# Three seven-product pairs in six of fifteen weight groups, and the other pairs at tiles 2 and 10

## The chip, the cores and the metric

The kernel runs on one core of a Trainium2 chip. The metric is the device time of one execution in microseconds (us). Names used below: TensorE (PE in the profile, PEld its weight loads), VectorE (DVE), ScalarE (ACT), GpSimd (POOL) and SyncE (SP), which issues the weight loads.

## The reference, cut to what matters

One encoder block on 256 tokens of width 2048, all in float32. The part that the change touches is the squared-ReLU MLP at the end:

```python
h = h + (g_mla * y_mla + g_fox * y_fox) @ w_out[l]
hn = rmsnorm(h, mlp_norm[l])
u = jnp.square(jax.nn.relu(hn @ w_up[l]))     # w_up: 2048 x 8192
h = h + u @ w_down[l]                         # w_down: 8192 x 2048
return rmsnorm(h, final_norm)
```

## The kernel before, in words

**Numbers in two parts.** Every operand of a product is split into a rounded part ("hi") and a rest ("lo"), and a product takes three matmuls: hi by hi, hi by lo, lo by hi (`three_passes`, L781 to L783). For a weight tile ScalarE writes hi (`unit_to_hi`, L1042) and VectorE then writes lo (`unit_to_lo`, L1318).

**Units and rings.** The weights are packed by the host as a stream of 456 units of 128 x 1024 values. SyncE loads them into a ring (`raw`, 4 slots, and from unit 208 on 8 slots with `raw_more`). hi and lo go to a ring `hl` of 4 slots, so hi of unit u starts only when TensorE has finished unit u-4. Each engine has a program written out by hand: VectorE and ScalarE walk over all units in order, and `make_due` lists, for each unit, which other work an engine does right after its own part of that unit. What is listed at a unit cannot overtake what stands ahead of it on its engine.

**Double groups.** The MLP is cut into four parts, each with two "up" groups (up0 0, up0 1, ...) and two "down" groups (the last part has one, then two ordinary groups). They are units 200 to 439: fifteen groups of 16 units, one 128-deep tile of the contraction per unit, and 1024 columns. For an ordinary tile TensorE computes four products (two token blocks by two column halves) into banks 0 to 3, twelve matmuls. The last two units of a group are worked block by block, and `block_left` and `unit_used` tell VectorE when each bank is finished.

**Seven-product pairs.** At the tiles named in `SEVEN` (4 and 10 before), two neighbouring tiles are taken together in Strassen's manner: seven products instead of eight, 21 matmuls instead of 24 (`seven_products`, L813). The order in it is: bank 7 and bank 5 (need the first two weight sums), bank 6 (third sum), bank 4 (needs unit k split), bank 1 (unit k), then banks 0 and 2 (need unit k+1 split). For a pair VectorE makes sums of the weight tiles (`weight_sums`, L1328, L1331, L1332), ScalarE their hi (`two_sums_to_hi` L1047, `third_sum_to_hi` L1052) and VectorE their lo (L1341). Both engines do this immediately ahead of their part of the pair's first unit. The sums have one buffer, which is free when bank 4's product of the previous pair is done. Sums of the activation rows of the pair's tiles are made once for each part (`row_sums`, L1353 to L1356, and hi and lo of them, L1126 and L1362), for the chunks of four tiles in `IN_CHUNK`, when these come back turned.

**The work after a group.** VectorE combines banks 4 to 7 at the group's units 14 and 15 ("products summed"; for down groups two more steps, at the next group's units 0 and 2). At the next group's unit 1 come the totals: `totals` (up) or `totals_into_resid` (down), the last of whose operations waits for the end of the group. After an up group ScalarE computes the squared ReLU of the two halves at the next group's unit 1 and unit 2 (`hidden_squares`, L1115 twice and L1120). VectorE transposes them in blocks at units 2 and 6 (`turn_hidden`, L1571), GpSimd sends each through HBM and back (L629, L636), and at units 8 and 12 they are split into `u_hl` (L1134, L1591), with row sums where the chunk has a pair.

**Start of the MLP.** Group up0 0 begins in banks 0 and 1, which the last w_out group has used. VectorE adds these to the residual in `take_tokens` (L1641), which is listed at unit 202, that is, after lo of unit 202.

Of the kernel before, what the change touches and what calls it, by code (L numbers as in the profile page):

```python
# [7 lines left out]
F32 = mybir.dt.float32  # L8
F32R = mybir.dt.float32r
# [67 lines left out]
        self.name, self.g = name, g  # L77


SEVEN = (4, 10)  # L80
IN_CHUNK = {k // 4: n for n, k in enumerate(SEVEN)}


def pairs_by_seven(name, g):

    return SEVEN


LAST_DOWN = f"down{MLP_PARTS - 1}"
# [138 lines left out]
def make_due():  # L228


    due = [[] for _ in range(N_UNITS)]

    def after(unit, what, g):
        due[min(unit + RING, N_UNITS - 1)].append((what, g))

    for gr in GROUPS:
        middle = gr.u0 + gr.units // 2 - 1
        if (gr.name, gr.g) in SCORES_IN:
            after(middle, "scored", SCORES_IN[gr.name, gr.g])
        if gr.name == "y_fox" and gr.g >= 2:  # L240
            after(middle, "mixed", 4 + gr.g)
        if gr.double:
            due[gr.u0 + 14].append(("p1 copied", gr))
            steps = (14, 15) if gr.name[:2] == "up" else (14, 15, 16, 18)
            for step, later in enumerate(steps):
                due[gr.u0 + later].append(("products summed", (gr, step)))
            due[gr.last + 2].append(("totals", gr))
        if gr.double and gr.name == LAST_DOWN:
            for c in range(2):
                due[gr.last + 3 + c].append(("chunk squared", Chunk(gr.name, 2 * gr.g + c)))  # L250
                due[gr.last + 5 + c].append(("chunk gained", Chunk(gr.name, 2 * gr.g + c)))
        if gr.name[:2] == "up":
            for c in range(2):
                piece = Chunk(gr.name, 2 * gr.g + c)
                piece.of, piece.c = gr, c
                due[gr.last + 2 + c].append(("hidden", piece))
                due[gr.last + 3 + 4 * c].append(("hidden turns", piece))
                due[gr.last + 9 + 4 * c].append(("u turned", piece))
                if piece.g in IN_CHUNK:
                    due[gr.last + 10 + 4 * c].append(("u summed", piece))  # L260
            if gr.n == 0:
                due[gr.u0 + 6].append(("mlp mean", gr))
                due[gr.u0 + 8].append(("mlp root", gr))
        if gr.double:
            continue
        if gr.name in ("y_mla", "w_out"):
            if gr.name == "w_out":
                after(gr.last + TURN_UNITS["w"] - 1, "h back", gr)
            after(gr.last + TURN_UNITS[gr.name[0]], {"y": "m turned", "w": "h turned"}[gr.name[0]], gr)
        if gr.name == "fq" and gr.g == 0:  # L270
            for later, what in ((2, "x norm"), (3, "latent norms"), (6, "keys rotated"), (9, "cq back"),
                                (10, "cq turned"), (14, "keys back"), (15, "keys turned"), (17, "forget exp"),
                                (18, "forget sums")):
                after(gr.u0 + later, what, gr)
        if gr is GROUPS[-1]:
            continue
        later = {("fq", 0): 5, ("fq", 1): 4, ("ukv_k", 0): 2, ("w_out", CHUNKS - 1): -1}.get((gr.name, gr.g), 0)
        after(gr.last + later - (gr.units == 1), "group", gr)
        if gr.name == "gates" and gr.g < 4:
            after(gr.last, "mixed", gr.g)  # L280
        elif gr.name == "gates" and gr.g == 7:
            after(gr.last, "mixed", 4)
        elif gr.name == "y_fox" and gr.g == 0:
            after(gr.last, "mixed", 5)
        elif gr.name in ("fq", "uq_nope"):
            after(gr.last + later + 8, "queries turned", gr)
        elif gr.name == "uq_rope":
            after(gr.last + 8, "queries rotated", gr)
            after(gr.last + 14, "queries turned", gr)
        elif gr.name == "fv" and gr.g == 1:  # L290
            after(gr.last, "scored", 0)
        elif gr.name == "ukv_v" and gr.g == 1:
            after(gr.last, "scored", 4)
    for work in due:
        work.sort(key=lambda it: not (it[0] == "group" and it[1].name == "w_out"))
    return due
# [45 lines left out]
def program(nc, stream, x_t, x_n, consts, gains, final_gain, cum_rows, prob_rows, turn_rows, out_n):  # L342
# [3 lines left out]
    def at(name, offset, *shape, dt=F32):  # L346
        return nc.alloc_sbuf_tensor_at(name, [P, *shape], dt, offset=sbuf0 + offset)
# [14 lines left out]
    prob_t = [at(f"prob_t{i}", o + offset * kib, 4, 2, 3, 32) for i, offset in enumerate((22, 15))]  # L362
    blocks = at("blocks", o + 19 * kib, TB * WIDE)
    hid = at("hid", o, 5, WIDE)
    sums = at("sums", o + 10 * kib, len(SEVEN), 4, 2, P)
    sums_hl = at("sums_hl", o + 10 * kib, len(SEVEN), 4, 2, P, dt=F32R)
    junk = at("junk", o + 23 * kib, WIDE)
    assert C_COUNT * 4 <= 8 * kib and G_COUNT * 4 <= 512
    A = o + 25 * kib
# [15 lines left out]
    m_hl = at("m_hl", B, KT, 2, T, dt=F32R)  # L385
    u_hl = at("u_hl", A, K_FF, 2, T, dt=F32R)
    raw_more = at("raw_more", B, DEEP_RING - RING, UNIT)
    u_sums = at("u_sums", B + 16 * kib, len(SEVEN), 4, 2, P)
    u_sums_hl = at("u_sums_hl", B + 16 * kib, len(SEVEN), 4, 2, P, dt=F32R)
    C = B + 32 * kib  # L390
    x_in = at("x_in", C, KT + KT * T)
    gate = at("gate", C, 2 * CHUNKS, TB, WIDE)
# [36 lines left out]
    with ctx:  # L429
# [110 lines left out]
        RIGHT_PIECES = [slice(2 * WIDE, 2 * WIDE + WIDE // 2), slice(2 * WIDE + WIDE // 2, 3 * WIDE),  # L540
                        slice(3 * WIDE, 4 * WIDE)]

        AHEAD_SUMS = {u for u in SEVEN_AT if u >= DEEP_FROM + DEEP_RING}

        def slot_of(u):
            return u % RING
# [15 lines left out]
        def sums_of(name):  # L562
            return {"up": sums_hl, "do": u_sums_hl}[name[:2]]
# [150 lines left out]
        def _(pe):  # L714
# [70 lines left out]
            def double_group(gr, tile, before_unit):  # L785
# [27 lines left out]
                def seven_products(k):  # L813

                    n = SEVEN.index(k)
                    last = k == gr.seven[-1]
                    sum_rows = lambda i: lambda part: sums_of(gr.name)[:, n, i, part]
                    sum_weights = lambda i: lambda part: (wsum_lo if part else wsum_hi)[:, i]
                    if gr.name == "up0":
                        pe.wait_ge(sums_split, n + 1)  # L820
                    elif gr.name[:2] == "do":
                        pe.wait_ge(sums_split, len(SEVEN) * (int(gr.name[4:]) + 1) + n + 1)
                    pe.wait_ge(wsum_split, 2 * SEVEN_AT[gr.u0 + k] + 1)
                    add_to(7, sum_rows(2), sum_weights(1), last)
                    add_to(5, sum_rows(0), sum_weights(0), last)
                    pe.wait_ge(wsum_split, 2 * SEVEN_AT[gr.u0 + k] + 2)
                    add_to(6, sum_rows(1), sum_weights(2), last)
                    pe.wait_ge(unit_split, gr.unit[k] + 1)
                    add_to(4, rows(k, 0), weights(k, 0), last).then_inc(seven_summed, 1)
                    add_to(1, rows(k + 1, 1), weights(k, 1)).then_inc(unit_used, 1)  # L830
                    pe.wait_ge(unit_split, gr.unit[k + 1] + 1)
                    add_to(0, rows(k + 1, 0), weights(k + 1, 1))
                    add_to(2, sum_rows(3), weights(k + 1, 0)).then_inc(unit_used, 1)
# [179 lines left out]
        def _(act):  # L1013
# [108 lines left out]
            def row_sums_to_hi(name, g):  # L1122

                n, (to, to_hl) = IN_CHUNK[g], ROW_SUMS[name[0]]
                act.wait_ge(sums_done, sums_before(name) + n + 1)
                nc.scalar.activation(to_hl[:, n, :, 0], to[:, n, :, 1], ACT.Copy).then_inc(sums_hi, 1)  # L1126

            def turned_to_hi(gr):
                back, dst, k0, tiles = turn_split(gr)
# [158 lines left out]
        def _(dve):  # L1288
# [55 lines left out]
            def row_sums(gr):  # L1344

                n, back = IN_CHUNK[gr.g], by_token(turned[:, SPLIT_NO[gr.name, gr.g] % 2])
                i = SEVEN[n] - 4 * gr.g
                to = lambda s: ROW_SUMS[gr.name[0]][0][:, n, s, 1].rearrange("p (a j) -> p a j", a=4)
                if gr.name in GAINED:
                    dve.wait_ge(turned_gained, GAINED[gr.name][0] + gr.g + 1)  # L1350
                else:
                    dve.wait_ge(turned_in, 4 * 16 * (TURN_NO[gr.name, gr.g] + 1))
                then_wait(nc.vector.tensor_tensor(to(0), back[:, i, 1], back[:, i + 1, 1], ALU.subtract))  # L1353
                nc.vector.tensor_tensor(to(2), back[:, i, 1], back[:, i, 0], ALU.subtract)
                then_wait(nc.vector.tensor_tensor(to(1), back[:, i, 0], to(0), ALU.subtract))
                nc.vector.tensor_tensor(to(3), back[:, i + 1, 0], to(1), ALU.subtract).then_inc(sums_done, 1)  # L1356

            def row_sums_to_lo(name, g):

                n, (to, to_hl) = IN_CHUNK[g], ROW_SUMS[name[0]]  # L1360
                dve.wait_ge(sums_hi, sums_before(name) + n + 1)
                nc.vector.tensor_tensor(to_hl[:, n, :, 1], to[:, n, :, 1], to_hl[:, n, :, 0].bitcast(F32),  # L1362
                                        ALU.subtract).then_inc(sums_split, 1)

            def sum_products(gr, step):
# [451 lines left out]
```

## Time and profile before

| | |
|---|---|
| median of 3 runs | 1267.52 us (1267.26 to 1268.73) |
| the profiled execution, as timed | 1264.23 us |
| its span in the trace | 1262.3 us |
| TensorE busy | 1250.6 us, 99% of the span, 5576 matmuls |
| TensorE weight loads busy | 1036.2 us, 82% |
| VectorE busy | 961.0 us, 76% |
| ScalarE busy | 670.4 us, 53% |
| GpSimd busy | 137.7 us, 11% |
| mean granted TensorE clock | 0.998 |

The profile is one execution. Its start-to-last-instruction span is 1.9 us shorter than its time, and its time is 3.3 us below the median of the runs. Busy time of an engine is the union of its instructions; the duration of one instruction can reach into the next one's, so the distance between starts tells more than the duration.

### The profile page before, as it was taken

What the parts mean: (1) busy time and instruction counts of PE and PEld (TensorE: products, weight loads), DVE (VectorE), ACT (ScalarE), POOL (GpSimd) and SP (SyncE); (2) the same over time, 40 slices, a digit from 0 to 9 for tenths busy, and PEclk for the clock granted to TensorE, in tenths of its full rate; (3) what the DMA queues carried; (4) which work ended last, traced back from release to release, by engine and by line L of the source; (5) the groups of instructions that cost most, each with busy time, mean ns of one, the idle gap of its engine ahead of it and who ended that gap; (6) DMA issues with size and microseconds to landing.
All of it is one profiled execution on the core that took longest, in us unless ns stands there. A gap on an engine that the chain in (4) does not pass through costs nothing.

```text
span 1262.3 us, 14832 instructions
## 1 busy us (share of the span) xinstructions
PE 1250.6 (99%) x5576; PEld 1036.2 (82%) x5576; DVE 961.0 (76%) x1057; ACT 670.4 (53%) x808; POOL 137.7 (11%) x239
## 2 busy tenths in 40 slices
PE   9999999999999999999999999999999999999997
PEld 7888888888888888887888888878888888888876
DVE  6676566646676677578899987889878897879884
ACT  6645345444555434455666445565455655456653
POOL 0021101103221112010001000110001110001100
PEclk9999999999999999999999999999999999999999
DMA  9788857765887779677787656766656786657761
GB/s 329 257 291 276 259 166 218 231 196 184 273 267 213 219 272 292 214 255 253 247 269 257 210 176 224 250 229 221 222 201 217 246 266 202 198 199 269 270 211 67
DMA packets 83143, 293.91 MB, mean 233 GB/s; under 512 B 11320, under 2 KB 12416, under 8 KB 82432
## 3 DMA queue, kind: packets, MB, share of 16 engines
q1 hardware_dynamic: 67536, 243.04, 58.0%
q0 software_dynamic: 14528, 48.00, 12.4%
q10 hardware_dynamic: 1008, 1.92, 0.5%
q8 instruction: 45, 0.74, 0.3%
q14 instruction: 26, 0.21, 0.0%
HBM read 269.45 MB, written 23.47 MB: 232 GB/s over the span
## 4 chain that ended last, share of the span: by engine, by line
PE 91%; DVE 3%; DMA 2%; issue 1%; ACT 1%; POOL 0%; DVEq 0%; ACTq 0%; POOLq 0%
PE bank L735 47%; PE bank L781 14%; PE bank L782 14%; PE bank L783 14%; DMA turn_rows<-blocks 1%; DVE hl L1318 1%; DMA turned<-turn_rows 1%; ACT hid L1115 1%; PE bank L924 1%; ACT hl L1042 1%; PE bank L906 0%; PE bank L904 0%; DVE wsum_lo L1341 0%; PE bank L948 0%; DVE wsum L1328 0%
## 5 line engine op out<-in xcount | busy, mean ns | idle before, releaser
L1318 DVE TENSOR_TENSOR hl<-raw,hl 128x1024 fp32r<-128x1024 f32 x327 | 398.4, 1233 | 195.6 <-ACT hl L1042 194.4
L1042 ACT ACTIVATE hl<-raw 128x1024 fp32r<-128x1024 f32 x327 | 341.5, 1056 | 330.8 <-PE bank L735 204.8
L735 PE MATMUL bank<-hl,x_hl 128*128 128x512 f32 (+1 forms) x1536 | 345.3, 385 | 0.0
L735 PEld LDWEIGHTS bank<-hl,x_hl 128*128 128x128 f32 x1536 | 283.9, 188 | 57.1 <-DVE hl L1309 0.9
L1318 DVE TENSOR_TENSOR hl<-raw_more,hl 128x1024 fp32r<-128x1024 f32 x124 | 147.7, 1218 | 30.2 <-ACT hl L1042 29.7
L781 PE MATMUL bank<-hl,hn_hl 128*128 128x512 f32 x432 | 168.4, 390 | 1.7 <-DVE resid L1641 1.4
L783 PE MATMUL bank<-hl,hn_hl 128*128 128x512 f32 x432 | 168.1, 389 | 0.0
L782 PE MATMUL bank<-hl,hn_hl 128*128 128x512 f32 x432 | 168.1, 389 | 0.0
L781 PE MATMUL bank<-hl,u_hl 128*128 128x512 f32 x378 | 147.3, 390 | 0.8 <-DVE u_hl L1591 0.7
L782 PE MATMUL bank<-hl,u_hl 128*128 128x512 f32 x378 | 147.1, 389 | 0.0
L783 PE MATMUL bank<-hl,u_hl 128*128 128x512 f32 x378 | 147.1, 389 | 0.0
L1042 ACT ACTIVATE hl<-raw_more 128x1024 fp32r<-128x1024 f32 x124 | 126.1, 1050 | 35.9 <-PE bank L783 29.9
L781 PEld LDWEIGHTS bank<-hl,hn_hl 128*128 128x128 f32 x432 | 81.1, 188 | 19.9 <-issue 2.9
L783 PEld LDWEIGHTS bank<-hl,hn_hl 128*128 128x128 f32 x432 | 81.1, 188 | 17.0
L782 PEld LDWEIGHTS bank<-hl,hn_hl 128*128 128x128 f32 x432 | 81.1, 188 | 16.7
L629 POOL DMA_DIRECT2D turn_rows<-blocks x35 | 19.7, 562 | 621.4 <-DVE blocks L1571 621.1
L735 PE MATMUL bank<-hl,m_hl 128*128 128x512 f32 x384 | 87.2, 389 | 0.0
L781 PEld LDWEIGHTS bank<-hl,u_hl 128*128 128x128 f32 x378 | 70.9, 188 | 16.5 <-DVE u_hl L1591 1.1
L735 PEld LDWEIGHTS bank<-hl,m_hl 128*128 128x128 f32 x384 | 72.1, 188 | 15.0
L783 PEld LDWEIGHTS bank<-hl,u_hl 128*128 128x128 f32 x378 | 71.0, 188 | 14.8
L782 PEld LDWEIGHTS bank<-hl,u_hl 128*128 128x128 f32 x378 | 70.9, 188 | 14.5
L1047 ACT ACTIVATE wsum_hi<-wsum 128x1024 fp32r<-128x1024 f32 x30 | 31.9, 1063 | 90.4 <-DVE wsum L1328 90.4
(227 smaller groups left out, 1335.4 us busy)
## 6 DMA issues: line engine op xcount, KB each, us to landing
raw<-weights SPq DMA_DIRECT2D x330, 512.0 KB, 4.4
raw_more<-weights SPq DMA_DIRECT2D x124, 512.0 KB, 4.6
turn_rows<-blocks POOLq DMA_DIRECT2D x34, 512.0 KB, 3.9
turned<-turn_rows POOLq DMA_DIRECT2D x96, 128.0 KB, 3.3
prob_rows<-prob_blocks POOLq DMA_DIRECT2D x8, 384.0 KB, 2.8
prob_t<-prob_rows POOLq DMA_DIRECT2D x32, 96.0 KB, 5.5
turned_h<-turn_rows POOLq DMA_DIRECT2D x20, 128.0 KB, 5.3
x_rows<-x_n POOLq DMA_DIRECT2D x2, 1024.0 KB, 8.6
```

The source lines that it names most:

```text
L629: pool.dma_start(turn_rows[n % 2, :, 0:4 * run], blocks[:, 0:4 * run]).then_inc(blocks_stored, 16)
L735: return nc.tensor.matmul(bank[:, gr.pair + tb, 0:gr.cols], tile[:, k, x_part, tb * P:tb * P + P], w, start=k == 0 and not x_part and not ...
L781: nc.tensor.matmul(bank[:, to], rows(0), w(0), start=first, stop=False)
L782: nc.tensor.matmul(bank[:, to], rows(0), w(1), start=False, stop=False)
L783: return nc.tensor.matmul(bank[:, to], rows(1), w(0), start=False, stop=last)
L924: nc.tensor.matmul(bank[:, 6, hh * T:hh * T + T], v[:, 0, cs], prob_t[n % 2][:, :, hh, 0:2].rearrange("p a k j -> p k a j"), start=True, s ...
L1042: nc.scalar.activation(hl[:, slot, 0], raw_unit(u), ACT.Copy).then_inc(unit_hi, 1)
L1047: nc.scalar.activation(wsum_hi[:, 0:2], wsum[:, 0:2], ACT.Copy).then_inc(wsum_rounded, 1)
L1115: ins = nc.scalar.activation(hid[:, 1 + 2 * c + tb], hid[:, 1 + 2 * c + tb], ACT.Relu, scale=rstd_col[:, MLP_NORM, tb:tb + 1])
L1318: nc.vector.tensor_tensor(hl[:, slot, 1], raw_unit(u), hl[:, slot, 0].bitcast(F32), ALU.subtract).then_inc(unit_split, 1)
```

## The change

`SEVEN` becomes (2, 6, 10). Groups up1 0, up2 0, up3 0 and down0 1, down1 1, down2 1 take all three pairs. The nine other double groups take two, at tiles 2 and 10 instead of 4 and 10. Row sums are made for chunks 0, 1 and 2 instead of 1 and 2, in separate buffers. The last step of a down group's products moves from the next group's unit 2 to its unit 4. In the last down group two squares and gains move by up to two units. `AHEAD_SUMS` leaves out the pairs at tile 2.

```diff
-SEVEN = (4, 10)
+SEVEN = (2, 6, 10)
+FEWER = (2, 10)
 IN_CHUNK = {k // 4: n for n, k in enumerate(SEVEN)}
 def pairs_by_seven(name, g):
-    return SEVEN
+    return SEVEN if (name[:2] == "up" and name != "up0" and g == 0) or (name[:4] == "down" and g == 1) else FEWER
...
-            steps = (14, 15) if gr.name[:2] == "up" else (14, 15, 16, 18)
+            steps = (14, 15) if gr.name[:2] == "up" else (14, 15, 16, 20)
...
-                due[gr.last + 3 + c].append(("chunk squared", Chunk(gr.name, 2 * gr.g + c)))
-                due[gr.last + 5 + c].append(("chunk gained", Chunk(gr.name, 2 * gr.g + c)))
+                due[gr.last + 3 + 3 * c].append(("chunk squared", Chunk(gr.name, 2 * gr.g + c)))
+                due[gr.last + 6 + c].append(("chunk gained", Chunk(gr.name, 2 * gr.g + c)))
...
-    sums = at("sums", o + 10 * kib, len(SEVEN), 4, 2, P)
-    sums_hl = at("sums_hl", o + 10 * kib, len(SEVEN), 4, 2, P, dt=F32R)
+    sums_at = (o + 10 * kib, o + 14 * kib, o + 85 * kib)
+    sums = [at(f"sums{n}", place, 4, 2, P) for n, place in enumerate(sums_at)]
+    sums_hl = [at(f"sums_hl{n}", place, 4, 2, P, dt=F32R) for n, place in enumerate(sums_at)]
...
-        AHEAD_SUMS = {u for u in SEVEN_AT if u >= DEEP_FROM + DEEP_RING}
+        AHEAD_SUMS = {gr.u0 + k for gr in DOUBLES for k in gr.seven if k > 2 and gr.u0 + k >= DEEP_FROM + DEEP_RING}
...
-                    sum_rows = lambda i: lambda part: sums_of(gr.name)[:, n, i, part]
+                    sum_rows = lambda i: lambda part: sums_of(gr.name)[n][:, i, part]
```

## Rows read from the trace of the kernel before

**Rows 1.** The page, busy time by engine.

```profile
PE 1250.6 (99%) x5576; PEld 1036.2 (82%) x5576; DVE 961.0 (76%) x1057; ACT 670.4 (53%) x808; POOL 137.7 (11%) x239
```

**Rows 2.** TensorE's waits: who waited for whom, total, times, longest (us).

```profile
PE bank L781 <- DVE resid L1641: 1.4, 1, 1.4
```

**Rows 3.** Timeline of TensorE, group up1 1: start, duration, line, instruction, count.

```profile
786.78 0.39 PE L781 MATMUL bank<-hl,hn_hl 128*128 128x512 f32 x1
...
797.66 0.39 PE L781 MATMUL bank<-wsum_hi,sums_hl 128*128 128x512 f32 x1
```

**Rows 4.** Timeline of VectorE, start of group up1 1, idle time before it in brackets.

```profile
786.98 0.69 DVE L1432 TENSOR_TENSOR hid<-bank,hid 128x512 f32<-128x512 f32 x1 [0.67 <-PE bank L783]
...
789.70 1.24 DVE L1571 STREAM_TRANSPOSE blocks<-hid 128x1024 f32<-128x1024 f32 x1
791.83 1.23 DVE L1318 TENSOR_TENSOR hl<-raw,hl 128x1024 fp32r<-128x1024 f32 x1 [0.89 <-ACT hl L1042]
792.97 1.22 DVE L1328 TENSOR_TENSOR wsum<-raw_more 128x1024 f32<-128x1024 f32 x1
...
795.68 1.83 DVE L1341 TENSOR_TENSOR wsum_lo<-wsum,wsum_hi 128x1024 fp32r<-128x1024 f32 x2
797.42 3.49 DVE L1318 TENSOR_TENSOR hl<-raw_more,hl 128x1024 fp32r<-128x1024 f32 x3
```

**Rows 5.** Timeline of ScalarE, the same stretch.

```profile
788.43 1.32 ACT L1115 ACTIVATE hid<-hid,rstd_col 128x512 f32<-128x512 f32 x2
789.79 1.06 ACT L1120 ACTIVATE hid<-hid 128x1024 f32<-128x1024 f32 x1
790.75 1.04 ACT L1042 ACTIVATE hl<-raw 128x1024 fp32r<-128x1024 f32 x1
...
796.21 3.89 ACT L1042 ACTIVATE hl<-raw_more 128x1024 fp32r<-128x1024 f32 x4
```

**Rows 6.** Timeline of VectorE and of TensorE at the start of the MLP.

```profile
571.35 2.44 DVE L1318 TENSOR_TENSOR hl<-raw,hl 128x1024 fp32r<-128x1024 f32 x2 [2.50 <-ACT hl L1042]
574.14 1.22 DVE L1641 TENSOR_TENSOR resid<-resid,bank 128x1024 f32<-128x1024 f32 x1 [0.35 <-PE bank L735]
...
575.50 0.47 PE L781 MATMUL bank<-hl,hn_hl 128*128 128x512 f32 x1 [1.40 <-DVE resid L1641]
```

**Rows 7.** VectorE's lo of a unit and the TensorE matmul that waited for it.

```profile
836.70 1.23 DVE L1318 TENSOR_TENSOR hl<-raw,hl 128x1024 fp32r<-128x1024 f32 x1 [0.89 <-ACT hl L1042]
...
838.07 0.47 PE L781 MATMUL bank<-hl,u_hl 128*128 128x512 f32 x1
```

**Rows 8.** Timelines of one block's way through HBM: GpSimd, VectorE, ScalarE.

```profile
791.50 0.56 POOL L629 DMA_DIRECT2D turn_rows<-blocks  x1 [107.11 <-DVE blocks L1571]
795.23 2.19 POOL L636 DMA_DIRECT2D turned<-turn_rows  x4 [3.17 <-DMA turn_rows<-blocks]
...
800.83 1.24 DVE L1571 STREAM_TRANSPOSE blocks<-hid 128x1024 f32<-128x1024 f32 x1
...
817.54 1.06 ACT L1134 ACTIVATE u_hl<-turned 128x1024 fp32r<-128x1024 f32 x1 [4.86 <-DMA turned<-turn_rows]
...
1140.44 1.24 DVE L1571 STREAM_TRANSPOSE blocks<-hid 128x1024 f32<-128x1024 f32 x1
...
1153.51 1.06 ACT L1134 ACTIVATE u_hl<-turned 128x1024 fp32r<-128x1024 f32 x1 [1.22 <-DMA turned<-turn_rows]
```

**Rows 9.** Timeline of VectorE, row sums of a chunk and the lo of its block.

```profile
849.09 0.28 DVE L1353 TENSOR_TENSOR u_sums<-turned 128x128 f32<-128x128 f32 x1
...
850.15 1.22 DVE L1591 TENSOR_TENSOR u_hl<-turned,u_hl 128x1024 fp32r<-128x1024 f32 x1
```

**Rows 10.** Windows, up0 1 and up2 0: length, busy time (instructions) by engine, clock, DMA.

```profile
618.20:660.30 42.10, 42.10 (x188) 34.85 (x186) 38.37 (x42) 26.69 (x31) 5.50 (x10) 1.00 0.75 248
1042.10:1084.20 42.10, 42.10 (x187) 34.88 (x186) 34.84 (x35) 20.09 (x21) 0.00 (x0) 1.00 0.62 202
```

**Rows 11.** Timeline of VectorE, a down group's last total.

```profile
873.62 0.69 DVE L1408 TENSOR_TENSOR resid<-resid,bank 128x512 f32<-128x512 f32 x1 [0.21 <-PE bank L783]
```

More of the change, by code:

```diff
@@ L387, in program @@
     raw_more = at("raw_more", B, DEEP_RING - RING, UNIT)
-    u_sums = at("u_sums", B + 16 * kib, len(SEVEN), 4, 2, P)
-    u_sums_hl = at("u_sums_hl", B + 16 * kib, len(SEVEN), 4, 2, P, dt=F32R)
+    u_sums_at = [B + (16 + 4 * n) * kib for n in range(len(SEVEN))]
+    u_sums = [at(f"u_sums{n}", place, 4, 2, P) for n, place in enumerate(u_sums_at)]
+    u_sums_hl = [at(f"u_sums_hl{n}", place, 4, 2, P, dt=F32R) for n, place in enumerate(u_sums_at)]
+    assert sums_at[-1] == B + 28 * kib
     C = B + 32 * kib
@@ L1125, in row_sums_to_hi @@
                 act.wait_ge(sums_done, sums_before(name) + n + 1)
-                nc.scalar.activation(to_hl[:, n, :, 0], to[:, n, :, 1], ACT.Copy).then_inc(sums_hi, 1)
+                nc.scalar.activation(to_hl[n][:, :, 0], to[n][:, :, 1], ACT.Copy).then_inc(sums_hi, 1)
             def turned_to_hi(gr):
@@ L1347, in row_sums @@
                 i = SEVEN[n] - 4 * gr.g
-                to = lambda s: ROW_SUMS[gr.name[0]][0][:, n, s, 1].rearrange("p (a j) -> p a j", a=4)
+                to = lambda s: ROW_SUMS[gr.name[0]][0][n][:, s, 1].rearrange("p (a j) -> p a j", a=4)
                 if gr.name in GAINED:
@@ L1361, in row_sums_to_lo @@
                 dve.wait_ge(sums_hi, sums_before(name) + n + 1)
-                nc.vector.tensor_tensor(to_hl[:, n, :, 1], to[:, n, :, 1], to_hl[:, n, :, 0].bitcast(F32),
+                nc.vector.tensor_tensor(to_hl[n][:, :, 1], to[n][:, :, 1], to_hl[n][:, :, 0].bitcast(F32),
                                         ALU.subtract).then_inc(sums_split, 1)
```

## The prediction, made before the changed kernel ran

> **What bounds the kernel now.** I read the busy time by engine first. TensorE is busy for 1250.6 of 1262.3 us [rows 1], and its list of waits is almost empty; the longest is one of 1.4 us, for the residual add ahead of the MLP [rows 2]. Then TensorE's timeline: in group up1 1 the pair at tile 4 starts 10.88 us after the group's first matmul, and four units of twelve matmuls lie between, so one matmul takes 10.88 / 48 = 0.2267 us from start to start [rows 3]. (The 0.39 us duration overlaps the next one.) A matmul taken away is worth 0.2267 us as long as nobody is late. Third, the windows by group: VectorE is busy for 38.4 of 42.1 us in an up 1 group, 34.8 in an up 0 group that follows a down group [rows 10]. TensorE bounds, but VectorE is close behind, so the question is where in a group the added VectorE work falls. That is read from the timelines of VectorE and ScalarE around a group's start.
>
> **The clock of a group.** Let S be the first matmul of a group. A unit lasts 12 x 0.2267 = 2.72 us, a pair 21 x 0.2267 = 4.76 us. In up1 1, S = 786.78 [rows 3], and VectorE's last total, which waits for the end of the group before, starts at 786.98 = S+0.20 [rows 4]. A down group's last total is also released by TensorE [rows 11].
>
> **Matmuls removed.** The new rule gives six groups three pairs and nine groups two: 36 pairs instead of 30. Each saves 3 matmuls: 18 x 0.2267 = -4.08 us, 5558 matmuls instead of 5576. The Trainium skill ("TensorE: Matmul & The Clock Gate", on sustained throughput) gives about 131 ns for a 512-column matmul in a stream, by which the saving would be 18 x 0.131 = 2.4 us. The trace does not agree: 227 ns.
>
> **Weight sums, their place.** Counted from the start t of L1328, lo of the sums starts at t+2.71 (795.68 - 792.97), lo of the pair's first unit at t+4.45, and ScalarE's hi of that unit at t+3.24 [rows 4, 5]. Lo operations of units in a row start 1.14 us apart (3.49 us for three). Before, t = S+6.2, with the pair due at S+10.88. Now the pair at tile 2 is due at S+5.44, and VectorE comes to its sums only after the last total, so t = S+0.20+0.60 = S+0.80 (0.60 us from start to start for 512 columns: the two lo of the sums take 1.83 us together, 1.14 of it up to the second's start, and the last 0.09 overlaps what follows). The `AHEAD_SUMS` edit moves nothing: both places in the loops are next to each other, with nothing between. The first sums are split by t+2.71+1.22 = S+4.73: in time, by 0.6 us. Unit 2 is split by t+4.45+1.23 = S+6.48; bank 4's product asks for it 9 matmuls into the pair, at S+7.48: in time.
>
> **Unit 3 after an up group: late.** On ScalarE the squares of the second half stand between hi of unit 2 and hi of unit 3. They take 2.32 us (788.43 to 790.75) and hi 1.04 [rows 5]; hi of unit 2 takes 0.95 us from start to start (3.89 us for four). So hi of unit 3 starts at t+3.24+0.95+2.32 = t+6.51 and ends at t+7.55, VectorE follows 0.04 later and ends at t+8.82 = S+9.62. TensorE asks for unit 3 after 15 matmuls of the pair, at S+5.44+3.40 = S+8.84. A matmul starts 0.14 us after the lo that it waited for (836.70+1.23 to 838.07) [rows 7], and the next is some 0.08 us late too. Stall: 9.62+0.14+0.08-8.84 = 1.0 us. Before, unit 3 was asked for at S+8.16 and ready at 791.83+1.23 = S+6.28 [rows 4], so the cover was 1.7 us and is gone. This comes in the four up 1 groups and the four down 0 groups: 4.0 + 4.0 us. After a down group ScalarE has no squares, lo of unit 3 ends at t+6.8 = S+7.6, and there is no stall.
>
> **The same groups, second half.** The transposition of the first half moves from S+2.92 to S+6.39. Its way to ScalarE took 13.1 us (1140.44 to 1153.51) to 16.7 us (800.83 to 817.54) for second halves, where ScalarE waited for it (shortest and longest of eight, mean 14.3); the store alone took 3.7 us for a first half (791.50 to 795.23) [rows 8]. I take 12.6, an estimate below the short end, since a first half's store starts 1.8 us after the transposition (791.50 - 789.70), now S+8.2, when only one weight load is under way ahead of it. It arrives at S+19.0. Between it and the sums for the pair at tile 10 stand the row sums of the chunk (1.06 us [rows 9]; new in the up 1 groups, down 0 groups had theirs), the lo of the block and of unit 9 (2 x 1.14) and the lo of the row sums (0.60): t = arrival+3.94, sums split at t+3.93, that is arrival+7.9 = S+26.9. The pair is due at S+26.5+1.0 = S+27.5. So each microsecond of the way beyond 13.1 is a stall of one, eight times over; below it nothing. The bounds are 0 and 8 x 3.6; I take 1.5 us in all. The Trainium skill ("DMA: Bandwidth & Descriptors", issuing engines are not separate DMA queues) says that transfers of SP and GpSimd run on the same 16 engines and interleave. The trace bears it out in the longer ways of second halves, and by it alone the way of first halves would lengthen towards theirs.
>
> In an up 1 group VectorE then has 38.4 + 1.7 us (1.06 + 0.60) of work and waits of its own in 43.1 us. I walk its queue to its last total at S+43.7 instead of S+43.4, which puts the next group's t 0.35 us later: 4 x 0.35 = 1.4 us more in the down 0 groups.
>
> **Three-pair groups: hidden.** They gain 4.45 us of VectorE work, to 39.3 of 41.5 us [rows 10]. The sums for tile 6 wait neither for the buffer (bank 4 of the pair at tile 2 is done at S+8.2) nor for data; VectorE comes to them at 0.80+4.45+4 x 1.14+1.14 (the moved step)= S+10.9, split at S+14.9, due at S+15.65. Cover 0.5 us after the restart, so nothing is charged; without the cover it costs what is missing, six times. The moved step costs nothing else: its banks are not asked for until unit 14.
>
> **The start of the MLP: late.** The residual add that frees banks 0 and 1 is listed at unit 202, and now the sums of the pair at 202 stand ahead of it on VectorE. Before, lo of 201 and 202 began at 571.35 and the add at 574.14, when TensorE was done [rows 6]. Now VectorE is free at 571.35+1.14 = 572.49, needs 4.45 us for the sums and 1.14 for lo of 202, and starts the add at 578.08: 3.94 us later, and TensorE with it. Queued behind it are the last transposition and the gains of chunk 2, whose users have more than 3.9 us. Bounds: 2.4 us, if unit 201 had not come late (VectorE had sat idle 2.50 us), and some 5 us if unit 203 is not there yet. I take 3.9, the rows as they are.
>
> The row sums of w_out's chunk 0 (1.7 us of VectorE at unit 192) and the moved squares at the end lie beside free time of their engines and cost nothing.
>
> **Sum.** -4.08 + 3.94 + 4.0 + 4.0 + 1.4 + 1.5 = +10.8 us. The profiled execution would go from 1264.2 to 1275.0. The median of the runs lies 3.3 us above it, 1267.5, so the median goes to 1278.3 us. A measurement of this kernel tells 0.2% (2.5 us) from no change.
>
> **Rivals.** (a) The way through HBM decides: the stores of first halves meet the weight loads that VectorE now releases in a bunch after unit 3. At the middle of second halves' ways, some 14.3 us, each of eight groups pays 1.2 us: 1278.3 - 1.5 + 9.6 = 1286; at 16.7 it would be 1306. For it: all eight second halves took 13.1 us or more. Against: the store of a first half has one load ahead of it, not four. (b) Faster: the chain to unit 3 is shorter than in the rows. It is 0.9 us too long; if VectorE's last total or ScalarE's squares came that much earlier against the pair, no group would stall, and if the residual add were ready too, only the saved matmuls would show: 1267.5 - 4.1 = 1263.4. It decides at S+8.7 for the end of lo of unit 3. For it: VectorE's work still fits in TensorE's time in every group. Against: each link is an order of a queue, and each duration has a row. (c) The groups hold but the MLP's start does not: 1263.4 + 3.9 = 1267.3, no change. (d) The change does not do what it says, with pairs fewer or sums moved by `AHEAD_SUMS`: the loops read plainly, and I give it nothing of its own.
>
> **How the numbers follow.** Forecast 0.65, (a) 0.14, (b) 0.08, (c) 0.09, others 0.04, mostly slower. The forecast's own range: low 1267.5-4.1+2.4+8 x 0.8 = 1272, high 1267.5-4.1+3.9+8 x 1.35+9.6 = 1288. To leave out no more than 2 in 10 I go from 1268 to 1289. Faster 0.08, same 0.10, slower 0.82.
>
> **What would show it.** TensorE: 5558 matmuls; its list of waits has L781 waiting for L1318 eight times, about 1 us each, 8.84 us after a group's start; the wait for L1641 grows from 1.4 to 5.3 us. ScalarE: hi of unit 3 about S+7.3 in those groups. The three-pair groups last 41.5 us with no gap. If TensorE shows no gap at unit 3, the queue walk is wrong; if gaps stand at unit 8 or at the pair at tile 10, the way through HBM is (a).

## The result, and the profile after

| | before | after |
|---|---|---|
| median of the runs | 1267.39 us | 1301.02 us (1298.71 to 1304.85, 4 runs) |
| ratio to before | | 1.0277, 95% interval 1.0248 to 1.0306 |
| profiled execution, span | 1262.3 us | 1296.8 us |
| TensorE matmuls | 5576 | 5558 |

The changed kernel is 2.8% slower. The direction was forecast, the size was not: +34 us instead of +11, outside the range.

The page of the changed kernel, busy time by engine, against [rows 1]:

```profile
PE 1258.8 (97%) x5558; PEld 1035.2 (80%) x5558; DVE 991.7 (76%) x1112; ACT 679.5 (52%) x825; POOL 138.1 (11%) x239
```

There are 18 matmuls fewer, and still TensorE is "busy" for 8 us longer, which is already a hint that some matmuls ran slower. Its list of waits (total, times, longest in us), against [rows 2]:

```profile
PE bank L785 <- DVE u_hl L1595: 9.1, 4, 4.0
PE bank L785 <- DVE hl L1322: 8.8, 11, 1.5
PE bank L785 <- DVE resid L1645: 6.0, 1, 6.0
PE bank L785 <- DVE wsum_lo L1345: 5.8, 4, 1.5
```

(Lines are 4 higher than before.) The third row and eight of the eleven waits of the second are steps of the forecast. The first row, the fourth and the other three waits of the second (at unit 9, 2.0 us together) are blocks that came back late from HBM. Five windows follow. The second is group up1 1, the third is most of the stretch in which the first half is read back in it, and the other three lie behind long waits (length, busy time and instructions by engine, granted clock, DMA share, GB/s):

```profile
580.10:585.40 5.30, 5.30 (x13) 4.14 (x14) 5.20 (x9) 3.97 (x7) 0.56 (x1) 0.50 0.49 192
801.10:846.20 45.10, 42.98 (x188) 34.58 (x187) 38.86 (x46) 25.68 (x29) 5.50 (x10) 1.00 0.65 215
815.50:822.40 6.90, 6.90 (x32) 5.73 (x31) 2.07 (x3) 0.80 (x2) 0.56 (x1) 1.00 1.00 308
872.40:876.00 3.60, 3.60 (x11) 2.77 (x10) 3.50 (x5) 1.92 (x3) 0.75 (x2) 0.53 0.93 269
1223.90:1227.60 3.70, 3.70 (x11) 2.84 (x11) 3.63 (x5) 1.06 (x1) 2.19 (x4) 0.54 0.62 187
```

VectorE, called close behind in the forecast, is busy for 38.9 of 45.1 us in up1 1, against 38.4 of 42.1 in the same kind of group before [rows 10]. It has hardly more work and stands idle for 6.2 us instead of 3.7: it is not overloaded, it waits.

**Where the 34.5 us are**, from the distances between starts of TensorE's matmuls, each less the regular 0.2267 us:

| place | forecast | measured |
|---|---|---|
| 18 matmuls | -4.1 | -4.1 |
| late residual add at the MLP's start | +3.9 | +4.6 |
| unit 3 of the pair at tile 2, eight groups, with VectorE's lateness in down 0 groups | +9.4 | +9.8 |
| units 8, 9 and 12 and the pair at tile 10, eight groups | +1.5 | +20.8 |
| matmuls at half the clock behind waits, three places | 0 | +5.8 |
| gaps that before had, gone from the same sum | 0 | -3.4 |

That is 33.5 us; 1 us is not assigned. In the six three-pair groups no distance is over by 0.06 us.

The chain of the forecast, seen in up1 1 of the changed kernel. VectorE and ScalarE from the group's start S = 801.13, then the two matmuls of TensorE that waited (answers to [rows 3] to [rows 5]):

```profile
801.33 0.69 DVE L1436 TENSOR_TENSOR hid<-bank,hid 128x512 f32<-128x512 f32 x1 [0.67 <-PE bank L787]
801.94 1.22 DVE L1332 TENSOR_TENSOR wsum<-raw 128x1024 f32<-128x1024 f32 x1
...
806.39 1.22 DVE L1322 TENSOR_TENSOR hl<-raw,hl 128x1024 fp32r<-128x1024 f32 x1
807.52 1.24 DVE L1575 STREAM_TRANSPOSE blocks<-hid 128x1024 f32<-128x1024 f32 x1
809.52 1.23 DVE L1322 TENSOR_TENSOR hl<-raw,hl 128x1024 fp32r<-128x1024 f32 x1 [0.76 <-ACT hl L1046]
...
822.38 0.29 DVE L1357 TENSOR_TENSOR u_sums<-turned 128x128 f32<-128x128 f32 x1 [4.83 <-DMA turned<-turn_rows]
...
826.36 1.22 DVE L1332 TENSOR_TENSOR wsum<-raw 128x1024 f32<-128x1024 f32 x1
```

```profile
806.13 1.32 ACT L1119 ACTIVATE hid<-hid,rstd_col 128x512 f32<-128x512 f32 x2
807.48 1.06 ACT L1124 ACTIVATE hid<-hid 128x1024 f32<-128x1024 f32 x1
808.45 1.04 ACT L1046 ACTIVATE hl<-raw 128x1024 fp32r<-128x1024 f32 x1
```

```profile
810.80 0.50 PE L785 MATMUL bank<-hl,hn_hl 128*128 128x512 f32 x1 [0.67 <-DVE hl L1322]
...
830.43 0.47 PE L785 MATMUL bank<-wsum_hi,sums_hl 128*128 128x512 f32 x1 [1.44 <-DVE wsum_lo L1345]
```

The sums begin at S+0.81 (forecast 0.80), the transposition at S+6.39 (6.39), lo of unit 3 at S+8.39 behind the squares (8.39), and its matmul waits. Then comes what failed: the first half, stored as fast as before, is back only at 822.38, 14.9 us after its transposition and not 12.6. From there the steps are again as worked out: sums at arrival+3.98, the matmul at arrival+8.05. In the four down 0 groups the block itself is late first, at unit 8 (1.7 to 4.2 us), and little or nothing is left to wait for at tile 10. GpSimd's rows, against [rows 8]:

```profile
809.32 0.56 POOL L633 DMA_DIRECT2D turn_rows<-blocks  x1 [110.41 <-DVE blocks L1575]
813.08 2.19 POOL L640 DMA_DIRECT2D turned<-turn_rows  x4 [3.20 <-DMA turn_rows<-blocks]
815.87 0.56 POOL L633 DMA_DIRECT2D turn_rows<-blocks  x1 [0.60 <-DVE blocks L1575]
```

The store takes 3.76 us. The four reads are issued until 815.27 and land 7.1 us later. From 815.5 to 822.4 the DMA engines are busy for 1.00 of the stretch. Before, the reads of the same block fell in 795.0 to 800.8, where the window of before says 0.68:

```profile
795.00:800.80 5.80, 5.80 (x27) 4.82 (x26) 5.77 (x6) 4.72 (x6) 2.19 (x4) 1.00 0.68 201
```

The traces also tell how many weight loads are under way between the issue of the first read and the landing of the last, here for the first half of up1 0, with two of the experiments below beside it:

| | before | after | e5 | e7 |
|---|---|---|---|---|
| weight loads under way | 2 | 6 | 4 | 3 |
| one read, issue to landing (us) | 2.7 to 2.8 | 5.5 to 7.6 | 3.8 to 5.7 | 2.6 to 5.0 |
| first read issued to last landed (us) | 4.4 | 9.3 | 7.3 | 6.6 |

Before, seven of the eight first halves were back 9.8 to 11.5 us after their transposition, and one, in down3 0, after 14.2. ScalarE took most of them up later than that, since it had other work first.

### The profile page after: what moved, and what is told of

Its sections match the earlier page's. It is cut to its first block, busy times and chain, and to the rows that moved or that the text cites. A ratio compares the mean times of both kernels' runs of the same rounds, so it can differ in the third digit from the quotient of the medians.

```text
span 1296.8 us, 14874 instructions
## 1 busy us (share of the span) xinstructions
PE 1258.8 (97%) x5558; PEld 1035.2 (80%) x5558; DVE 991.7 (76%) x1112; ACT 679.5 (52%) x825; POOL 138.1 (11%) x239
## 4 chain that ended last, share of the span: by engine, by line
PE 74%; DVE 14%; DMA 8%; issue 2%; POOL 1%; ACT 0%; DVEq 0%; POOLq 0%; ACTq 0%
PE bank L739 43%; PE bank L785 10%; PE bank L787 10%; PE bank L786 10%; DMA turned<-turn_rows 5%; DVE hl L1322 4%; DMA turn_rows<-blocks 2%; DVE wsum_lo L1345 2%; DVE wsum L1332 1%; DVE u_hl L1595 1%; POOL turned L640 1%; DVE blocks L1575 1%; DVE raw L1336 1%; DVE wsum L1335 1%; PE bank L928 1%
## 5 line engine op out<-in xcount | busy, mean ns | idle before, releaser
L785 PE MATMUL bank<-hl,hn_hl 128*128 128x512 f32 x417 | 164.3, 394 | 10.7 <-DVE resid L1645 6.0
L787 PE MATMUL bank<-hl,hn_hl 128*128 128x512 f32 x417 | 163.3, 392 | 0.0
L786 PE MATMUL bank<-hl,hn_hl 128*128 128x512 f32 x417 | 163.2, 391 | 0.0
L785 PE MATMUL bank<-hl,u_hl 128*128 128x512 f32 x363 | 143.8, 396 | 13.2 <-DVE u_hl L1595 9.1
L786 PE MATMUL bank<-hl,u_hl 128*128 128x512 f32 x363 | 142.6, 393 | 0.0
L787 PE MATMUL bank<-hl,u_hl 128*128 128x512 f32 x363 | 142.6, 393 | 0.0
L785 PEld LDWEIGHTS bank<-hl,hn_hl 128*128 128x128 f32 x417 | 78.9, 189 | 30.8 <-issue 9.9
L1051 ACT ACTIVATE wsum_hi<-wsum 128x1024 fp32r<-128x1024 f32 x36 | 38.2, 1060 | 113.6 <-DVE wsum L1332 113.6
L785 PEld LDWEIGHTS bank<-hl,u_hl 128*128 128x128 f32 x363 | 68.9, 190 | 32.0 <-DVE u_hl L1595 11.7
L787 PEld LDWEIGHTS bank<-hl,hn_hl 128*128 128x128 f32 x417 | 78.8, 189 | 16.7
L786 PEld LDWEIGHTS bank<-hl,hn_hl 128*128 128x128 f32 x417 | 79.0, 189 | 16.1
L739 PEld LDWEIGHTS bank<-hl,m_hl 128*128 128x128 f32 x384 | 71.9, 188 | 15.4 <-DVE hl L1322 0.3
L787 PEld LDWEIGHTS bank<-hl,u_hl 128*128 128x128 f32 x363 | 68.9, 190 | 14.7
L786 PEld LDWEIGHTS bank<-hl,u_hl 128*128 128x128 f32 x363 | 69.0, 190 | 14.0
```

What stands on the lines that cost most here:

```text
L739: return nc.tensor.matmul(bank[:, gr.pair + tb, 0:gr.cols], tile[:, k, x_part, tb * P:tb * P + P], w, start=k == 0 and not x_part and not ...
L785: nc.tensor.matmul(bank[:, to], rows(0), w(0), start=first, stop=False)
L786: nc.tensor.matmul(bank[:, to], rows(0), w(1), start=False, stop=False)
L787: return nc.tensor.matmul(bank[:, to], rows(1), w(0), start=False, stop=last)
L1051: nc.scalar.activation(wsum_hi[:, 0:2], wsum[:, 0:2], ACT.Copy).then_inc(wsum_rounded, 1)
```

## The experiments

All start from the changed kernel, and each was timed beside the kernel before, whose medians there were 1263.0 to 1264.5 us (1267.4 above); so ratios compare better than times. "Way" is the time from the transposition of a first half to its use on ScalarE; in the changed kernel ScalarE waited for all eight, and they took 14.9 to 17.5 us, mean 15.6.

**e1_pairs_6_10.**

```diff
-FEWER = (2, 10)
+FEWER = (6, 10)
```

> The changed kernel with one line other: the nine two-pair groups take their pairs at tiles 6 and 10 instead of 2 and 10 (so none of them has a pair at tile 2; the six three-pair groups, the buffers and the row sums of chunk 0 stay; 36 pairs as in the changed kernel). Theory 1, the place of the pair at tile 2 costs everything and the three-pair groups cost nothing: no gap at unit 3, at unit 8 or at tile 10, no late residual add; the saved matmuls remain, some 1263.5 us beside about 1267.4 before. Theory 2, VectorE is simply overloaded by the six more pairs and the row sums of chunk 0, wherever they stand: the time stays well above before, 1275 or more, with gaps in the three-pair groups.

Measured: 1261.05 us, ratio 0.9965 (0.9950 to 0.9979). It beats both kernels, the one before by 0.35%. TensorE's waits:

```profile
PE bank L785 <- DVE u_hl L1595: 1.5, 2, 0.9
PE bank L785 <- DVE resid L1645: 1.4, 1, 1.4
```

The matmuls saved, the row sums of chunk 0 and all three-pair groups are the same as in the changed kernel. Only the pair at tile 2 behind an up group, and in up0 0, is gone, and with it the loss. Theory 2 (VectorE overloaded) falls. The ways are not short here: 12.6 to 15.4 us, mean 14.3, with 5 loads under way in up1 1. But they start at S+2.9 and not at S+6.4, so nearly all are in time.

**e2_squares_later.**

```diff
-                due[gr.last + 2 + c].append(("hidden", piece))
+                due[gr.last + 2 + 2 * c].append(("hidden", piece))
```

> The changed kernel with ScalarE's squares of the second half listed one unit later, after hi of unit 3 instead of after hi of unit 2. The gaps at unit 3 (0.8 us in up 1 groups, 1.2 us in down 0 groups, 8 in all, about 9 us with the restarts) should vanish. Theory 1, the way of the first half through HBM is fixed to the group's start and decides later in the same group: TensorE comes 1 us sooner to unit 8 or to the pair at tile 10 and waits there 1 us longer, so the time stays within 2 us of the changed kernel (1301). Theory 2, the gaps add up independently: 1292 us.

Measured: 1304.58 us, ratio 1.0313 (1.0287 to 1.0340). The gaps at unit 3 are gone in five of the eight groups and shrink to 0.3 us in three down 0 groups, and a gap of 0.4 us at unit 4 has come in all eight. Nothing is gained: TensorE waits longer for the first half instead, up to 6.2 us in one group. The list of waits:

```profile
PE bank L785 <- DVE u_hl L1595: 12.9, 4, 6.2
PE bank L785 <- DVE hl L1322: 9.4, 13, 4.0
```

Theory 1 holds, with 3.6 us more than the changed kernel rather than within 2 (the two intervals overlap): the ways were longer too, 16.4 us in the mean. The two kinds of gap are in series on one clock, the group's start, and the later one decides.

**e3_second_half_later.**

```diff
-                due[gr.last + 3 + 4 * c].append(("hidden turns", piece))
+                due[gr.last + 3 + 6 * c].append(("hidden turns", piece))
```

> The changed kernel with the transposition of the second half moved from unit 6 to unit 8, so that its store to HBM starts after the first half's reads are back. In the changed kernel the first half's store takes 3.8 us, but its reads land 7.1 us after the last of them is issued, with the second half's store issued 0.6 us behind them. Theory 1, that store slows the reads: they land in 3 to 5 us, the way takes some 12.5 us instead of 15.6, and the gaps at unit 8 and at the pair at tile 10 go (minus 12 to 18 us), though second halves may come late to unit 12 in the four down 0 groups (plus 0 to 6). 1285 to 1292 us. Theory 2, the bunch of weight loads slows them: the way stays at 15 us and the time at 1300 or above.

Measured: 1313.91 us, ratio 1.0384 (1.0354 to 1.0414). The second half's store now starts after the first half is back (here reads at 817.20, arrival 827.63, next store 831.67):

```profile
817.20 2.19 POOL L640 DMA_DIRECT2D turned<-turn_rows  x4 [3.20 <-DMA turn_rows<-blocks]
831.67 0.56 POOL L633 DMA_DIRECT2D turn_rows<-blocks  x1 [12.28 <-DVE blocks L1575]
```

Yet the ways of first halves still take 16.2 us in the mean. My first theory, that this store slows the reads, falls. The time rises because the second transposition (1.14 us) now stands between the arrival and the sums for tile 10, and the ways are 0.6 us longer: 8 x 1.7 = 14 us, where 13 were measured. The sum is not the whole account: the trace also has second halves late at unit 12 in three groups (0.3 to 0.7 us each) and more stretches at half the clock, some of which use up time that would have been waited anyway.

**e4_up0_pairs_6_10.**

```diff
-    return SEVEN if (name[:2] == "up" and name != "up0" and g == 0) or (name[:4] == "down" and g == 1) else FEWER
+    return SEVEN if (name[:2] == "up" and name != "up0" and g == 0) or (name[:4] == "down" and g == 1) else (6, 10) if (name, g) == ("up0", 0) else FEWER
```

> The changed kernel with only group up0 0 having its pairs at tiles 6 and 10 instead of 2 and 10, so that no weight sums stand ahead of the residual add. Theory 1, the late add cost 4.6 us of waiting and then 13 matmuls at half the clock (13 x 0.2 = 2.7 us), granted clock 0.50 in the stretch after it: the wait for the residual add goes from 6.0 back to 1.4 us, the clock stays at 1.00, and the time falls by 7.3 us to some 1293.7. Theory 2, the half clock comes from the start of the MLP and not from the wait: the time falls by 4.6 us, to 1296.4, and the slow matmuls stay.

Measured: 1295.57 us, ratio 1.0240 (1.0212 to 1.0268). The wait for the residual add is 1.4 us again, and the clock behind it is full:

```profile
575.60:581.00 5.40, 5.40 (x24) 4.46 (x25) 5.30 (x9) 4.98 (x8) 0.56 (x1) 1.00 0.55 213
```

Unit 3 of up0 1 is asked for 6.9 us sooner in this trace (626.9 against 633.8), near the 7.3 of theory 1, so the slow matmuls came with the wait. The time alone does not tell the theories apart: it fell by 5.4 us by the medians and 4.7 by the ratios, between the two and nearer to theory 2. In the profiled executions the lead shrinks to 1.6 us, since this one met longer waits for late blocks (11.8 us in all against 9.1; 5.2 against 4.0 in down3 0).

**e5_paced_loads.**

```diff
                     sp.wait_ge(unit_split, RAW_BEFORE[u] + 1)
+                if u >= DEEP_FROM + DEEP_RING:
+                    sp.wait_ge(unit_used, u - 8)
                 sp.dma_start(raw_unit(u), stream[u]).then_inc(unit_loaded[RAW_SLOT[u]], 16)
```

> The changed kernel, where SyncE issues each weight load from unit 216 on only when TensorE has also finished the unit 9 before it, so that loads go out at TensorE's pace and not in a bunch when VectorE catches up. In the changed kernel the 16 DMA engines are busy for 1.00 of the stretch in which the first half's reads are under way (0.68 before the change), and those ways took 14.9 to 17.5 us. Theory 1, the bunch of weight loads slows the reads: the ways fall to 11 to 13 us, the gaps at unit 8 and at the pair at tile 10 shrink from 18 us in all to under 6, the time to 1285 to 1290. Theory 2, the reads are slow for another reason (their small packets, the queue that GpSimd writes): the ways stay at 15 us, the time at 1300.

Measured: 1283.13 us, ratio 1.0151 (1.0126 to 1.0175), 16 to 18 us less than the changed kernel. Seven ways took 12.8 to 13.8 us and one 16.1. Waits for late blocks and late sums fall from 14.9 to 4.4 us, the waits at unit 3 stay:

```profile
PE bank L787 <- DVE hl L1324: 6.8, 8, 1.0
...
PE bank L787 <- DVE u_hl L1597: 3.7, 3, 2.6
...
PE bank L787 <- DVE wsum_lo L1347: 0.7, 2, 0.6
```

Only the issue of weight loads was changed, so it is the loads that VectorE releases in a bunch that slow the reads. A fixed cost of this way, or small packets, would have left it at 15 us. Pacing takes away part of the slowness and not all: four loads are still under way during the reads in up1 1, and the ways are 13.6 us in the mean.

**e6_pairs_6_10_paced.** The kernel of e1 with e5's pacing.

> The kernel with the nine two-pair groups at tiles 6 and 10 (1261.05 us), with the same pacing of the weight loads. Two gaps of 0.8 and 1.1 us at late blocks were left in it. If the bunch of loads slows the ways, the ways get shorter than 14.3 us in the mean and the gaps go: 1259. If a load now comes late to a pair's sums, which need two units ahead of time, a gap for a load shows in VectorE's waits: 1265 or more.

Measured: 1272.06 us, ratio 1.0058 (1.0038 to 1.0078): 11 us worse than e1. The ways of first halves got only 0.7 us shorter (13.5 us in the mean, after 14.3), those of second halves got longer (16.0 us after 14.1, up to 17.8), and TensorE waited for late blocks for 5.8 us in all and for lo of units for 3.0 us more. VectorE waited once for a load (1.5 us). A pace that helps where loads were bunched pushes them into the next block's way where they were not.

**e7_first_half_earlier.**

```diff
-                due[gr.last + 3 + 4 * c].append(("hidden turns", piece))
+                due[gr.last + 2 + 5 * c].append(("hidden turns", piece))
```

> The changed kernel with VectorE's transposition of the first half listed at unit 1, ahead of the weight sums of the pair at tile 2 instead of behind them and lo of unit 2. Its way through HBM starts 5.5 us sooner against the group's start; the sums and all that follows them come 1.2 us later. Theory 1 (the start of the way decides): the gaps at unit 8 and at the pair at tile 10 vanish (minus 18 us), the gaps at unit 3 grow by 1.2 each (plus 10), the pair at tile 2 itself waits some 0.6 (plus 5): about 1298. Theory 2 (VectorE's total work decides and the way only shows it): the late gaps stay, and the time goes to 1312 or more.

Measured: 1279.82 us, ratio 1.0124 (1.0103 to 1.0146). Every late gap is gone:

```profile
PE bank L785 <- DVE hl L1322: 8.5, 8, 1.2
PE bank L785 <- DVE resid L1645: 6.4, 1, 6.4
PE bank L785 <- DVE wsum_lo L1345: 2.8, 5, 0.6
```

No wait for `u_hl` is left. ScalarE takes the first halves up 15.4 us after their transposition, but it does not wait for them; its own order puts them there, as in up1 1 (transposition at 796.51):

```profile
810.92 1.06 ACT L1046 ACTIVATE hl<-raw 128x1024 fp32r<-128x1024 f32 x1 [1.66 <-PE bank L787]
811.89 1.04 ACT L1138 ACTIVATE u_hl<-turned 128x1024 fp32r<-128x1024 f32 x1
```

The blocks were back after 11.2 to 12.1 us in seven groups and after 14.2 in down3 0. So two things changed: the way starts 5.5 us sooner, and its reads fall outside the bunch of loads. The start alone would have been enough, by an estimate from these rows: S+0.8 and a way of 15.6 give S+16.4, where S+19.5 is in time. That the late gaps vanish is theory 1; the time is 18 us below my number, and the fault is in my sum: the pair at tile 2 now waits 0.7 us, and this is part of what unit 3 would have waited, so the gaps at unit 3 are 1.2 to 1.3 us and not 2.2, and the half clock behind late blocks (3.1 us) goes too. I had also priced the late gaps at 18 us where they were 20.8.

**e8_all_three.** e7, e2 and e4 at once.

> The changed kernel with three edits at once: the transposition of the first half at unit 1, ScalarE's squares of the second half one unit later, and up0 0 with its pairs at tiles 6 and 10. The pairs at tile 2 stay in the eight groups that follow an up group. If the late residual add with its half clock (7.3 us), the squares ahead of unit 3 (9) and the late start of the way through HBM (18) are all there is, only the first weight sums of the pair at tile 2 still come late, by 0.6 to 0.8 us in eight groups: 1301 - 34 + 6 = 1273 us. If VectorE's overall load matters beside them: 1280 or more.

Measured: 1271.18 us, ratio 1.0054 (1.0033 to 1.0074). The number is met within 2 us, and the three causes taken away leave no late gap. But it is met in part by luck. With the pairs at tile 2 kept, 0.6 to 0.7 us in each of eight groups stays for the first weight sums, as worked out, and 0.8 to 1.0 at unit 4, some 7 us in all, which was not. That is made up for by the late gaps, which had cost 20.8 us and 3.1 at half the clock, and not 18. The kernel stays slower than before.

**e9_two_pairs_everywhere.**

```diff
-    return SEVEN if (name[:2] == "up" and name != "up0" and g == 0) or (name[:4] == "down" and g == 1) else FEWER
+    return FEWER
```

> The changed kernel without the third pairs: all fifteen groups have two, at tiles 2 and 10 (30 pairs, 5576 matmuls, as before the change; buffers and row sums as in the changed kernel). Theory 1, the six third pairs are free work for VectorE and earn 18 matmuls: 4.1 us slower than the changed kernel, some 1305 us, a ratio of 1.031 to before. Theory 2, their VectorE work delays the groups that follow: the time is the changed kernel's or less, a ratio of 1.028 or under.

Measured: 1304.56 us, ratio 1.0319 (1.0295 to 1.0343). The difference to the changed kernel's 1.0277 is 0.0042, or 5 us, against 4.1 worked out; the two intervals overlap, so the times alone do not show it. The traces do: the six groups with three pairs last 41.48 us each, and 42.16 here with two, with no gap in either. The third pairs earn their matmuls.

**e10_6_10_half_earlier and e11_6_10_again.** The kernel of e1 with e7's edit, and the kernel of e1 once more.

> The kernel with the two-pair groups at tiles 6 and 10, and the transposition of the first half at the group's unit 1 instead of behind lo of unit 2. If the gaps left in that kernel (0.8 and 1.1 us at late blocks) come from the start of the way through HBM, they vanish and it runs at 1.5 to 2 us less than it; if they come from VectorE's order at unit 2, lo of unit 2 now comes late and nothing is gained. Ratio to before 0.995 against 0.9965.

> The kernel with the two-pair groups at tiles 6 and 10, again beside the other two and in more rounds: 36 pairs against 30 and no gap of weight sums should be worth 18 x 0.2267 = 4.1 us less than before, a ratio of 0.9968; it measured 0.9965.

Measured: e10 1259.76 us, ratio 0.9960 (0.9944 to 0.9975); e11 1261.72 us, ratio 0.9971 (0.9959 to 0.9982). Both beat the kernel before, by 0.3 to 0.4%. Whether the earlier transposition adds anything to it is inside the intervals; in e10's trace one long wait for a late block is left (2.7 us, in down3 0), in e11's four of 1.4 us and less. The traced execution of e10 took 1265.99 us, 6 us above its median, so its long wait need not be typical.

## Why the prediction was wrong in size

**Right.** The matmul price (0.2267 us) and their number. That the residual add comes late behind the pair at unit 202: 4.6 us for 3.9, the rest because unit 201's load was 0.6 us later in this execution. The chain to unit 3: forecast 1.0 us, measured 0.93 in up 1 groups (0.83 and 0.10 at the next matmul), and 0.35 more in down 0 groups by VectorE's late totals, as walked. The pair at tile 2 waits 0.2 us itself there, which the walk did not have. Three-pair groups free. The `AHEAD_SUMS` edit moves nothing: the orders on VectorE and ScalarE are as read.

**The step that failed** is "The same groups, second half": the term of 1.5 us measured 20.8. Its mechanism and its threshold (a way of 13.1 us) were right: (15.6 - 13.1) x 8 = 20 us. In up1 1, say, the way of 14.86 us makes 1.76 of stall by this rule, and 1.84 were measured. The size of the way was wrong, 12.6 instead of 15.6. I took it from the short end because "only one weight load is under way ahead" of the store. That was so, and the store took 3.76 us as before; but I looked at the store alone. The four reads that follow start 3.8 us after the store, in the middle of the loads that VectorE releases when it catches up: its lo of units 3 to 8 start within 6.8 us (809.52 to 816.34), where TensorE needs 2.72 for each unit. The reads are issued in 2.19 us as before, and take 9.3 us to be back instead of 4.4. This is rival (a), to which I gave 0.14, and the sign that I had named for it, gaps at unit 8 and at the pair at tile 10, is there. I priced even it at a mean way of 14.3 us, from second halves of before, though the bunch is denser after the change. e5 shows the cause, e1 and e7 that the start of the way against the group's start decides, and e3 that the ways are no shorter without the other half's store. What stays open is the longest way, 17.5 us in down3 0: GpSimd takes 4.8 us to issue its four reads there, before the change too, and no run shows why.

The Trainium skill ("DMA: Bandwidth & Descriptors", issuing engines are not separate DMA queues) was cited in the prediction: SP's and GpSimd's transfers share the same 16 engines, by which the ways of first halves would lengthen. It was the better guide here than my choice of row; e5 bears it out by the move from 15.6 to 13.6 us in the mean with nothing but SP's issues changed.

**The term that was missing**: the clock. After the 6 us wait at the MLP's start TensorE ran at 1.2 GHz (granted 0.50 in 580.10 to 585.40), 13 matmuls 0.43 us apart, 2.7 us; and twice more behind late blocks, 3.1 us. My working priced a wait at its length and put nothing for this.

## What to carry to other kernels

When a piece of work is moved later on an engine that runs ahead of the bound, price not only the wait it creates but what the engine does when it catches up: it hands back its buffers in a bunch, and every transfer that the following work waits for has to pass through that bunch. For a round trip through memory look at each leg in its own time window, the reads as well as the store, and read the DMA share there. A place that holds many waits in series against one start should be tested by moving the last one, since removing an early one gives nothing while a later one stands (e2).

## What the runs showed of the hardware

**A wait of TensorE can cost more than its length.** Behind the 6.0 us wait 13 matmuls ran at half the clock, behind one of 4.0 us 8 did, with three at full speed in between. Behind the 1.8 us wait at 870.84 the clock fell 1.5 us after the restart; the 1.8 us wait at 696.38 was followed by none. In e8 the wait at the MLP's start was 1.8 us and the mean clock after it 0.67:

```profile
575.90:581.00 5.10, 5.09 (x15) 4.05 (x16) 5.00 (x9) 3.98 (x7) 0.56 (x1) 0.67 0.68 227
```

In the kernel before, in e1 and in e4 this wait was 1.4 us, with no fall. These runs do not show which waits are followed by a fall.

**The same 512 KB to HBM and back** took 10.0 to 10.3 us for the second halves of e3, with 3 weight loads under way during the reads, and 15.4 to 17.8 us for its first halves, with 6. The windows of up1 1's reads, the first half's and then the second half's:

```profile
817.20:827.60 10.40, 10.40 (x48) 8.61 (x47) 3.44 (x3) 1.55 (x2) 2.19 (x4) 1.00 0.98 299
835.60:840.10 4.50, 3.29 (x15) 2.76 (x16) 4.50 (x5) 3.31 (x4) 2.18 (x4) 1.00 0.62 178
```
